# Gather edge reordered and MLP norm factor moved into the last norm's epsilon, in one two-block kernel

## What is computed

```python
def peer_ffn(h, w_pq, subkeys, u, v):
    q = (h @ w_pq).reshape(b, s, 8 heads, 2, 128)
    ...                                   # top 16 of 128 subkeys on each side, top 16 of the 256 sums
    act = gelu(einsum('chkd,cd->chk', u[expert], h)) * softmax(gates)
    return einsum('chk,chkd->cd', act, v[expert])      # 8 heads x 16 experts a token, rows of 1024
...
    h2 = rmsnorm(x, pre_norm_mlp[l])
    y = jnp.square(jax.nn.relu(h2 @ w_up[l])) @ w_down[l]
    x = x + rmsnorm(y, post_norm_mlp[l])
```

## Time and profile before

| | |
|---|---|
| median of 3 runs | 1448.82 us |
| the profiled execution, its span | 1448.1 us, 1446.2 us |
| PE busy | 1312.6 us, 91% |
| DVE busy | 949.7 us, 66% |
| ACT busy | 497.3 us, 34% |
| POOL busy | 455.6 us, 32% |
| gather traffic | 268.45 MB in the queue of indirect DMAs |
| mean granted TensorE clock | 0.970 of full |

### The profile page before, as it was taken

How to read it: one execution, slowest core, us unless ns; L and a number is a source line. 1 busy time by engine, 2 the same in 40 slices (tenths; PEclk the granted TensorE clock), 3 DMA queues, 4 the chain that set the end, 5 groups by cost and what they waited for, 6 DMA issues and landing times.

```text
span 1446.2 us, 25078 instructions
## 1 busy us (share of the span) xinstructions
PE 1312.6 (91%) x9606; PEld 1234.7 (85%) x9606; DVE 949.7 (66%) x2086; ACT 497.3 (34%) x973; POOL 455.6 (32%) x325
## 2 busy tenths in 40 slices
PE   9999999999999886877878896879899999899997
PEld 8999999988889886877868786879786789789996
DVE  4689987665685676859595868655416547656665
ACT  5533456445233121212112221211225456443433
POOL 1588722000225554554535354546003000000000
PEclk9999999999999999998999898999999999999999
DMA  7555554552589999999999999999930135245551
GB/s 277 197 193 178 179 181 170 175 197 111 217 345 396 426 426 427 428 428 428 427 427 426 426 427 427 428 426 427 399 147 30 41 106 184 94 161 189 179 199 59
DMA packets 57895, 397.91 MB, mean 275 GB/s; under 512 B 6352, under 2 KB 9040, under 8 KB 10192
## 3 DMA queue, kind: packets, MB, share of 16 engines
q0 software_dynamic: 36864, 268.45, 44.2%
q1 hardware_dynamic: 20944, 128.28, 24.9%
HBM read 395.66 MB, written 1.05 MB: 274 GB/s over the span
## 4 chain that ended last, share of the span: by engine, by line
PE 57%; DMA 21%; DVE 10%; issue 7%; ACT 3%; POOL 1%; DVEq 0%; POOLq 0%; ACTq 0%
DMA rows_late<-peer_uv_dram,stage 20%; PE bank L751 11%; PE bank L752 11%; PE bank L753 11%; PE bank L1008 7%; PE bank L714 6%; PE bank L735 5%; DVE rows_late L2073 3%; ACT w_hi L1230 1%; POOL rows_late L656 1%; PE bank L873 1%; DVE w_lo L544 1%; PE bank L897 1%; PE bank L963 1%; PE bank L856 0%
## 5 line engine op out<-in xcount | busy, mean ns | idle before, releaser
L1008 PE MATMUL bank<-h_norm,rows_late 128*128 128x128 f32 x2816 | 326.4, 278 | 27.5 <-ACT h_norm L1424 27.5
L1008 PEld LDWEIGHTS bank<-h_norm,rows_late 128*128 128x128 f32 x2816 | 322.5, 195 | 30.6 <-ACT h_norm L1424 30.6
L2073 DVE SCALAR_TENSOR_TENSOR rows_late<-rows_late,squares 128x1024 f32<-128x1024 f32 x176 | 213.1, 1228 | 118.7 <-DMA rows_late<-peer_uv_dram,stage 112.3
L1008 PE MATMUL bank<-h_norm,rows_early 128*128 128x128 f32 x1280 | 170.3, 299 | 79.0 <-ACT h_norm L1424 79.0
L1008 PEld LDWEIGHTS bank<-h_norm,rows_early 128*128 128x128 f32 x1280 | 165.0, 213 | 84.5 <-ACT h_norm L1424 84.4
L656 POOL DMA_INDIRECT rows_late<-peer_uv_dram,stage x165 | 193.4, 1172 | 136.4 <-PE bank L1008 79.6
L544 DVE TENSOR_TENSOR w_lo<-raw,w_hi 128x2048 fp32r<-128x2048 f32 x66 | 151.3, 2294 | 102.7 <-ACT w_hi L1230 99.0
L1230 ACT ACTIVATE w_hi<-raw 128x2048 fp32r<-128x2048 f32 x94 | 178.9, 1904 | 57.4 <-PE bank L753 49.4
L751 PE MATMUL bank<-x_hi_a,w_hi 128*128 128x256 f32 x672 | 190.9, 284 | 2.7 <-DVE x_lo_a L1640 1.8
L752 PE MATMUL bank<-x_lo_a,w_hi 128*128 128x256 f32 x672 | 190.1, 283 | 0.0
L753 PE MATMUL bank<-x_hi_a,w_lo 128*128 128x256 f32 x672 | 190.1, 283 | 0.0
(11 more groups left out here) (355 smaller groups left out, 1888.0 us busy)
## 6 DMA issues: line engine op xcount, KB each, us to landing
raw<-w_in_dram SPq DMA_DIRECT2D x28, 1024.0 KB, 4.9
raw<-w_up_dram SPq DMA_DIRECT2D x16, 1024.0 KB, 4.9
raw<-w_down_dram SPq DMA_DIRECT2D x16, 1024.0 KB, 4.8
rows_late<-w_in_dram SPq DMA_DIRECT2D x10, 1024.0 KB, 13.4
raw<-w_kv_dram SPq DMA_DIRECT2D x8, 1024.0 KB, 4.9
rows_late<-w_peer_q_dram SPq DMA_DIRECT2D x5, 1024.0 KB, 12.2
raw<-sc_w_out_dram SPq DMA_DIRECT2D x4, 1024.0 KB, 4.7
raw<-cf_w_pw_dram SPq DMA_DIRECT2D x4, 1024.0 KB, 4.8
```

The source lines that it names most:

```text
L1008: mm = nc.tensor.matmul(ct(Y_ACC[c][t // 4], t % 4, P), expert_rows(k)[:, D + t * P:D + (t + 1) * P], ct(diag, k % DIAGS, P), start=False, ...
L2073: w_.scalar_tensor_tensor(out=row, in0=row, scalar=1.0, in1=h_tok[:, c * D:(c + 1) * D], op0=ALU.mult, op1=ALU.mult, accum_out=pre[:, side ...
```

## The change

In the gather: the first weights of head 0 are computed before `choose`; PE adds head 0's rows 0 to 3 behind query 5, rows 4 to 7 behind query 6 and rows 8 to 11 behind query 7; POOL issues four gathers of head 1 before k = 14 and four more before k = 15 of head 0; the diagonal tiles have storage of their own, `diag`; and the first whole load waits for the last row to have landed. `row_pad` shrinks by the 16 words that two small new tensors take, so all row slots and ring slots keep their addresses; `alibi` changes places with `v_b` and `o_a`.

In the MLP: the factor r = 1/sqrt(m + EPS) of the norm before it is left out of the up tiles. The hidden tile is then 1/r^2 times too large, and so is y; the norm behind takes that out if its epsilon is EPS times (m + EPS)^2. This is `up_eps`, one number a token, which ACT computes as (sqrt(EPS) m + EPS^1.5)^2 from m by token. So the mean square is summed by token, the reciprocal on DVE goes, and relu has no second factor. The first down pair comes before up pair 2, the transposes of x behind it; the last two up loads stand side by side with down pair 13 behind them; ACT rounds load f + 1 before hidden tile f; the last load is subtracted behind the last tile.

```diff
@@ plan()
+DOWN_BEHIND = {0: (), **{b: (b - 1,) for b in range(1, FH - 2)}, FH - 2: (), FH - 1: (FH - 3, FH - 2, FH - 1)}
     for b in range(FH):
         add("w_up_2", [b], "up", 2, "dve", 2 * b)
-        if b == 1:
+        if b == 2:
             other("xtok", 4, "act")
-        if b:
-            p.append(("w_down_2", b - 1, [], "dve"))
-    p.append(("w_down_2", FH - 1, [], "dve"))
+        for d in DOWN_BEHIND[b]:
+            p.append(("w_down_2", d, [], "dve"))
@@ storage
-        sb("row_pad", 64)
+        eps_cubed_root = sb("eps_cubed_root", 1)
+        up_eps = sb("up_eps", NC)
+        sb("row_pad", 48)
-        square_gains, diag = h_norm[:, 0:D], h_norm[:, D:D + DIAGS * P]
+        square_gains = h_norm[:, 0:D]        # diag is ("diag", DIAGS * P, F32) behind "weight"
@@ SP, load_whole
                 else:
+                    if n == 0:
+                        sp.wait_ge(rows_landed[TOPK - 1], NC * PH * 16)
                     sp.wait_ge(rows_free, ...)
@@ POOL
-            gathers(0, expert, first=True)
+            gathers(0, expert, range(TOPK - 2), first=True)
             pool.wait_ge(experts_known, 1)
-            gathers(1, stages[1])
+            stage_head(1, stages[1])
+            for n in range(2):
+                gathers(1, stages[1], range(n * GROUP, (n + 1) * GROUP))
+                gathers(0, expert, [TOPK - 2 + n], first=True)
+            gathers(1, stages[1], range(2 * GROUP, TOPK))
@@ PE, stat_beside
-                mm = nc.tensor.matmul(STAT[:, 0:SEQ], mean_d[:], ct(squares, k), start=(k == 0), stop=(k == DT - 1))
+                for c in range(NC):
+                    mm = nc.tensor.matmul(STAT[:, c:c + 1], ct(squares, k)[:, c * P:(c + 1) * P], mean_d[:, 0:1],
+                                          start=(k == c == 0), stop=(k == DT - 1 and c == NC - 1))
@@ PE, gather
-            for n in range(5, PH):
-                queries(n)
+            queries(PH - 3)
             ...
             pe.sem_inc(rows_free, DIAGS)
             bracket(0, True)
-            add_rows(0, 0, range(TOPK - GROUP))
+            for n in range(3):
+                add_rows(0, 0, range(n * GROUP, (n + 1) * GROUP))
+                if n < 2:
+                    queries(PH - 2 + n)
@@ PE, MLP
             for b in range(2, FH):
-                for f in (2 * b - 4, 2 * b - 3):
-                    ...
-                mm.then_inc(down_done, 1)
+                if b < FH - 1:
+                    down_pair(b - 2)
                 linear("up", range(2 * b, 2 * b + 2), "w_up_2", b, "mlp", DT, 256)
+                if b == 2:
+                    x_by_token()
+            down_pair(FH - 3)
@@ ACT, gather
-            drain_queries(5, 6, 7)
             ...
-            head(0, 0, which=slice(0, 3))
+            for n in range(3):
+                head(0, 0, which=slice(n, n + 1))
+                drain_queries(PH - 3 + n)
@@ ACT, MLP
-            root("mlp")
+            act.wait_ge(stat_ready, NORM_AT["mlp"] + 1)
+            s.activation(up_eps[:], STAT[:, 0:NC], ACT.Square, scale=EPS ** 0.5, bias=eps_cubed_root[:, 0:1]).then_inc(rooted, 1)
             for f in range(2 * FH):
+                round_to(LOAD_OF["up", 0] + f + (1 if f < 2 * FH - 2 else 0))
                 act.wait_ge(hid_ready, f + 1)
                 ...
                 s.activation(ct(hid_hi, f % FH), ct(hid, f % 4), ACT.Copy).then_inc(x_hi_ready, 1)
-                for n in range(4 if f == 3 else 0):
+                for n in range(4 if f == 5 else 0):
                     drain("xtok", n, ct(x_tok, n, 512), width=512)
-                round_to(LOAD_OF["up", 0] + f + 1)
@@ DVE, products
                     if k == choose_at:
+                        weigh(0, 0, GROUP)
                         for _ in pieces:
                             pass
@@ DVE, MLP
-            rstd_of("mlp")
-                dve.wait_ge(*freed(w_.scalar_tensor_tensor(out=turns[:], in0=acc("up", f), scalar=0.0,
-                                                           in1=rstd[:], op0=ALU.max, op1=ALU.mult)))
+                dve.wait_ge(*freed(w_.tensor_scalar(turns[:], acc("up", f), 0.0, None, ALU.max)))
                 ...
-                subtract_to(LOAD_OF["up", 0] + f + 1)
+                if f < 2 * FH - 2:
+                    subtract_to(LOAD_OF["up", 0] + f + 1)
             hid_low(2 * FH - 1)
+            subtract_to(len(LOADS))
```

More of the change, by code:

```diff
@@ L239 @@
     SPLIT_ENDS[_name] = _n
-SCALED = ("xa", "mlp")
+SCALED = ("xa",)
 BY_TOKEN = ("mix", "peer", "post_mix")
@@ L641, in _, with stage_head, gathers @@
             subtract_to(BEFORE_GATHERS)
-            def gathers(head, stage_at, first=False):
-                if not first:
-                    g.tensor_copy(stage_at, expert[:, bass.ds(head * TOPK, TOPK)]).then_inc(staged, 1)
-                    pool.wait_ge(staged, head)
-                for k in range(TOPK):
+            def stage_head(head, stage_at):
+                g.tensor_copy(stage_at, expert[:, bass.ds(head * TOPK, TOPK)]).then_inc(staged, 1)
+                pool.wait_ge(staged, head)
+            def gathers(head, stage_at, ks=range(TOPK), first=False):
+                for k in ks:
                     if first:
@@ L1176, in _, with x_by_token @@
                 mm.then_inc(down_done, 1)
+            def x_by_token():
+                pe.wait_ge(residual_added, DT)
+                for n in range(4):
+                    c, part = divmod(n, 2)
+                    out = open_tile("xtok", n)
+                    for j in range(4):
+                        mm = nc.tensor.transpose(out[:, j * P:(j + 1) * P], x_piece(c, 4 * part + j), ident)
+                    mm.then_inc(acc_ready, 1)
+            pe.wait_ge(rooted, len(ROOTS))
+            for b in range(2, FH):
+                if b < FH - 1:
+                    down_pair(b - 2)
                 linear("up", range(2 * b, 2 * b + 2), "w_up_2", b, "mlp", DT, 256)
+                if b == 2:
+                    x_by_token()
+            down_pair(FH - 3)
             for c in range(NC):
```

36 lines of the change are left out of this document (16 added, 20 removed).

## The result

The changed kernel takes 1430.89 us (median of 4 runs, 1430.28 to 1431.20), the kernel before 1448.53 (4 runs, 1446.97 to 1449.0) beside it on the same chip. The profiled execution has a span of 1428.7 us and a mean clock of 0.971, against 1446.2 before. Of its 17.5 us, 5.4 are there by the end of the gather, where 11.1 were forecast, and 12.1 are won in the MLP, forecast 12.2. The edits of the gather are worth the other 3.9. So the MLP's terms hold and the gather's two do not.

The account below looks back on a forecast made before the run. DMA engines bound the gather, PE the stretch from 1258 us on. Gains 6.2 + 4.9 + 7.7 + 4.5 = 23.3 took the profiled 1448.1 to 1424.8, plus 0.7 for the median: 1425.5 us, range 1420.5 to 1431.5.

Parts of the forecast that it names:

- The MLP's start: From the first up tiles through the third up pair and transposes: 7.7 us gained, bounds 8.3 and 3.
- Its end: MLP's last sums, with down pair 13 placed ahead of them: 4.5 us gained, bounds 4.6 and 2.
- The middle: MLP's middle: odd tiles' hid_hi up to 1.0 us later, hidden behind a down pair; no cost.
- C: MLP: PE stalls anew at the third up pair or last subtract, losing 6 us; 1431.5; chance 0.11 together with E.
- D: MLP, hid_hi of each odd tile: ACT's rounding sits on every pair's loop, adding 32.5 us; 1458; chance 0.03.
- E: MLP start: stalls were the norm's, so only the reciprocal's 1.75 us go; 1431.4; chance 0.11 together with C.
- a row costs 21.44/24 = 0.89 us: Gather: PE's time to add one expert row, put at 0.89 us.
- the last edge: End of the gather: whole loads wait, last product starts at 1031.4, not 1036.39; 4.9 us gained, bounds 5.2 and 0.6.
- the first edge: Gather's head: idle DMA time falls from 9.3 to 3.1 us; 6.2 us gained, bounds 9.3 and 2.
- rival A: First gather edge gives 2 us only, as the queue dries again after 446; 1429.7; chance 0.13.
- rival B: Last gather edge: whole-weight loads come late, PE waits, taking back 4.3 of 4.9 us; 1429.8; chance 0.09.

Follow-up runs that it names:

- e5: The changed kernel with the norm factor put back in the MLP, keeping the new order of pairs and transposes; 1433.91 us, ratio 0.9903.
- e1: The kernel before with the MLP part alone (new order, no norm factor, rounding ahead of its tile), gather unchanged; 1436.59 us, ratio 0.9921.
- e7: The changed kernel with ScalarE's rounding of the next load moved back behind the up tile's hid_hi; 1439.06 us, ratio 0.9942.
- e4: The changed kernel with the last head's weights for rows 4 to 11 made in groups of two, not four; 1430.08 us, ratio 0.9877.
- e9: The changed kernel with last-head weights in twos for rows 4-11, singly from 12, and head 0's rows 4-7 weighed behind product 8, not 9; 1428.95 us.
- e2: The kernel before with only the new order at the first gather edge, no wait on SP; 1446.05 us, ratio 0.9981.
- e3: The kernel before with only SP's first whole load waiting until the last expert row has landed; 1446.76 us, ratio 0.9985.

## Why the prediction was right and where it was not

**Direction, range, MLP: right.** The MLP's start is worth 7.7 us, as forecast: from up tile 3's end to the point where the third up pair and the transposes are both done it took 21.31 us (1257.98 to 1279.29) and now takes 13.64 (1252.62 to 1266.26). Its end is the other 4.4 of the 12.1, forecast 4.5: the last 72 matmuls run 0.227 us apart without a stop. The middle costs nothing. e5 and e1 bear this out, and rivals C, D and E fall: the one new wait, 0.66 us for the first hid_lo, was in the sum with 0.62, and nothing is paid per pair. What my working did not say is that order on ScalarE and on PE need each other. It treated ScalarE's edit as a cost hidden by a down pair, and in e7 it carries 8.6 us.

**The step that failed: "a row costs 21.44/24 = 0.89 us".** The 192 records of the earlier trace rows are 16 a row (8 products of f32, two records each), so they were 12 rows, 1.79 us each. Both gather terms used it. For the last edge e4 and e9 show what follows from it; for the first it is worked out from the timelines, since no run makes a row cheaper.

At the first edge I let PE catch up within 3.6 us per group, found it waiting 5.2 us for DVE's choice, and stopped counting idle bins at 447. In fact the group takes 7.2. Row 4's weights come as forecast (PE takes them 15.6 us behind the bracket's end, 15.7 reckoned), but query 6 starts 3.6 us later behind the bracket than reckoned, so the wait shrinks to 1.35, and the lower clock that I charged for it does not come: the rows behind it keep 1.8 us, at a granted clock of 1.00. Up to 448 the bins lack 3.8 us, where I had 3.1. Behind 448 I counted nothing, and they lack 3.2 more. PE is full and has no slack: the stream is thin to 454, and 1.5 us are missing at 460 to 462, for k = 15's weight. The term was 6.2 and is 1.7 by the profiles (2.8 by e2's runs). That is rival A, given 0.13: its 2 us, and its mechanism (the queue dries again after 446). What I set against it, that rows 8 to 11 are free right behind query 7, was true; rows 12 to 15 were what held up the queue.

At the last edge the landing was right to 0.04 us, and no load was late, so rival B falls. The text took the last product for the end. Behind it PE had eight rows to add. At 0.89 us, eight rows are 7.1 us and end at 1027.7, before the last row's product starts; at 1.79 they are 14.3, from 1020.60 to 1034.9, and the last row has landed by 1028.2. Term 4.9, measured 2.2 (e3), and e4 and e9 give the missing 2.2 to 2.7 back by feeding PE earlier.

In sum: 12.2 - 12.1, 6.2 - 1.7 and 4.9 - 2.2 are 7.3 us too many by the parts. The whole missed by only 5.7 us, and that it lies inside the range is luck: 1448.53 less the 16.0 of the parts is 1432.5, above the range's 1431.5, and the difference is of the size by which profiles with one and the same code differ before query 5. The range let each rival come true alone; here rival A's shortfall and 2.7 us at the last edge came together.

## What to carry to other kernels

Divide a run of matmul records by the rows of code that issue them before you price one: f32 products stand in the trace as two records each. Where a wait goes away, ask what the next engine on the path has queued: PE needs its inputs in small enough groups near an end, or it turns a transfer won into a backlog. And where two engines pass a load to and fro (rounding, subtract, tile), put the work that waits for nobody first; the loop's time per load against the bound's (here 10.7 against 11.2 us a pair) says that it keeps up in the middle, not at the ends of the loop, where the tiles come closer together. And before two profiles are compared, measure in each from one step that both have: here 1.5 of 5.4 us lay ahead of the edits.
